# A gated recurrence computed in two halves of channel blocks, with its gate products, exponentials and the next projection in another order

## The reference

```python
u, g = jnp.split(h @ w_in, 2, axis=-1)
u = causal_depthwise_conv(u, conv_w) + conv_b          # 4 taps
r  = sigmoid(block_diag(u, w_a) + b_a)                 # forget gate
gi = sigmoid(block_diag(u, w_x) + b_x)                 # input gate
log_a = -8.0 * r * softplus(-lam)
a = exp(log_a)
b_in = sqrt(-expm1(2.0 * log_a)) * (gi * u)
hs = scan over tokens of  h = a * h + b_in
x = x + gate * ((hs * silu(g)) @ w_out)
```

## Time and profile before

| | us |
|---|---|
| median of 3 runs | 1071.15 |
| the runs | 1072.08, 1065.59, 1071.15 |
| the profiled execution | 1070.5 |
| its span, first to last instruction | 1068.7 |
| PE busy | 950.9 (89%) |
| DVE busy | 751.5 (70%) |
| ACT busy | 469.9 (44%) |
| POOL busy | 96.6 (9%) |

### The profile page before, as it was taken

How to read it: one execution, slowest core, us unless ns; L and a number is a source line. 1 busy time by engine, 2 the same in 40 slices (tenths; PEclk the granted TensorE clock), 3 DMA queues, 4 the chain that set the end, 5 groups by cost and what they waited for, 6 DMA issues and landing times.

```text
span 1068.7 us, 12457 instructions
## 1 busy us (share of the span) xinstructions
PE 950.9 (89%) x4385; PEld 744.1 (70%) x4385; DVE 751.5 (70%) x1061; ACT 469.9 (44%) x728; POOL 96.6 (9%) x134
## 2 busy tenths in 40 slices
PE   3799986989999999899887999999958968998986
PEld 1588664766888888676566788888747856776765
DVE  0697497688768777865388877677779397784464
ACT  1542356444343343443254443443455764544461
POOL 0000010113001000100030001010000400100000
PEclk8799998898999999899988999999989989999998
DMA  9977164267998889545025698998825353764001
GB/s 355 375 258 255 40 224 147 82 228 253 343 323 286 310 292 303 189 145 155 3 80 197 232 344 290 309 295 297 313 79 197 110 191 133 261 250 158 1 1 40
DMA packets 115814, 222.91 MB, mean 209 GB/s; under 512 B 7146, under 2 KB 63180, under 8 KB 115770
## 3 DMA queue, kind: packets, MB, share of 16 engines
q1 hardware_dynamic: 92608, 141.57, 38.3%
q0 software_dynamic: 20992, 80.13, 22.0%
q10 hardware_dynamic: 2170, 0.64, 0.3%
HBM read 221.27 MB, written 1.05 MB: 208 GB/s over the span
## 4 chain that ended last, share of the span: by engine, by line
PE 71%; DVE 15%; ACT 5%; issue 4%; DMA 2%; POOL 1%; ACTq 0%; POOLq 0%; DVEq 0%; SPq 0%
PE bank L1668 20%; PE bank L1670 19%; PE bank L1669 19%; DVE w_lo L1016 4%; ACT w_hi L533 2%; DMA w_land<-ev_w_in_dram 2%; DVE job_sum L1033 1%; PE bank L2195 1%; PE bank L1725 1%; DVE tmp L1103 1%; DVE x L1104 1%; PE bank L1894 1%; PE bank L2029 1%; POOL x L489 1%; DVE xfull L1142 1%
## 5 line engine op out<-in xcount | busy, mean ns | idle before, releaser
L1668 PE MATMUL bank<-w_hi,xT_hi 128*128 128x512 f32 x816 | 337.9, 414 | 31.6 <-DVE xT_lo L1126 14.1
L1016 DVE TENSOR_TENSOR w_lo<-w_land,w_hi 128x2048 fp32r<-128x2048 f32 x124 | 283.4, 2289 | 99.0 <-ACT w_hi L533 98.7
L1669 PE MATMUL bank<-w_lo,xT_hi 128*128 128x512 f32 x816 | 326.8, 401 | 0.0
L1670 PE MATMUL bank<-w_hi,xT_lo 128*128 128x512 f32 x816 | 326.4, 400 | 0.0
L533 ACT ACTIVATE w_hi<-w_land 128x2048 fp32r<-128x2048 f32 x124 | 236.9, 1912 | 135.2 <-PE bank L1670 132.0
L1668 PEld LDWEIGHTS bank<-w_hi,xT_hi 128*128 128x128 f32 x816 | 159.1, 195 | 72.6 <-issue 27.5
L1670 PEld LDWEIGHTS bank<-w_hi,xT_lo 128*128 128x128 f32 x816 | 158.7, 194 | 35.1
L1669 PEld LDWEIGHTS bank<-w_lo,xT_hi 128*128 128x128 f32 x816 | 159.4, 195 | 32.2 <-issue 1.0
L1033 DVE SCALAR_TENSOR_TENSOR job_sum<-a_land,silu_c,job_sum 128x1024 f32<-128x1024 f32 x126 | 164.2, 1303 | 6.6 <-DMA a_land<-mod_w_dram 3.1
L1668 PE MATMUL bank<-w_hi,hT_hi 128*128 128x512 f32 x176 | 70.4, 400 | 1.0 <-DVE w_lo L1016 1.0
L1670 PE MATMUL bank<-w_hi,hT_lo 128*128 128x512 f32 x176 | 68.7, 390 | 0.0
(11 more groups left out here) (291 smaller groups left out, 1051.3 us busy)
## 6 DMA issues: line engine op xcount, KB each, us to landing
...
```

The costliest lines, as they stand in the source:

```text
L1016: dve.tensor_tensor(w_lo[u % N_SPLIT][:, :], w_land[n % N_LAND][:, :], w_hi[u % N_SPLIT][:, :].bitcast(F32), ALU.subtract).then_inc(s_lo, 1)
L1668: pe.matmul(dst, hi, whi, start=start, stop=False)
L1669: pe.matmul(dst, hi, wlo, start=False, stop=False)
L1670: return pe.matmul(dst, lo, whi, start=False, stop=stop)
```

## The change

- The four groups of the forget gate come first in RG_GROUPS, then the four of the input gate.
- The eight exponentials follow the second pair of forget groups. The input gate is computed as tanh of half the argument, with a halved bias (half_bias, one small DVE instruction), in place of a sigmoid; DVE forms (tanh+1)*uc, and the root is taken of a quarter of its argument, which brings the missing half.
- POOL no longer multiplies the input gate by uc, and squares a for all eight blocks; DVE squares none.
- The silu of chunk 2 is applied as it leaves the banks. `split_hi` of base+9 comes before `rg_rows(3)`.
- DVE and ACT take blocks 0 to 3 through root product, scan, silu product and split, then the gate's diagonal, then blocks 4 to 7, with `split_lo` of base+9 between their scans and their outputs.
- PE does the first unit of rg_out for tile 0 before the transposes of chunk 3, tile 1 after them. Writing banks 4 and 5 in `gate_mm` waits for the last silu.

```diff
-RG_GROUPS = [(0, 0), (0, 1), (1, 0), (1, 1), (0, 2), (0, 3), (1, 2), (1, 3)]
+RG_GROUPS = [(0, 0), (0, 1), (0, 2), (0, 3), (1, 0), (1, 1), (1, 2), (1, 3)]
...
         sp_c = small("sp_c", [P, 8, KT])
+        half_bias = place("half_bias", [P, KT], FOUR_G)
...
             for k in range(KT):
-                pool.wait_ge(sem("rg_sig"), rg_sigs(1, k))
-                pool.tensor_tensor(i_gate[:, k, :], i_gate[:, k, :], uc[:, k, :], ALU.mult).then_inc(sem("rg_iu"), 1)
-            for k in range(0, KT, 2):
                 pool.wait_ge(sem("rg_a"), k + 1)
...
                     k = 2 * h + e
-                    dst, b = ((r_gate, "rg_b_a_2"), (i_gate, "rg_b_x_2"))[n]
-                    act.activation(dst[:, k, :], bank[6 + g % 2][:, 256 * e:256 * e + 256], ACT.Sigmoid,
-                                   bias=pc(b, k)).then_inc(sem("rg_sig"), 1)
+                    src = bank[6 + g % 2][:, 256 * e:256 * e + 256]
+                    if n == 0:
+                        ins = act.activation(r_gate[:, k, :], src, ACT.Sigmoid, bias=pc("rg_b_a_2", k))
+                    else:
+                        ins = act.activation(i_gate[:, k, :], src, ACT.Tanh, scale=0.5, bias=half_bias[:, k:k + 1])
+                    ins.then_inc(sem("rg_sig"), 1)
                 if n == 0:
...
             split_hi(base + 7)
-            for g in range(2, 6):
+            for g in range(2, 4):
                 rg_sigmoids(g)
+            for k in range(KT):
+                act.wait_ge(sem("rg_th"), k + 1)
+                act.activation(r_gate[:, k, :], r_gate[:, k, :], ACT.Exp, scale=sp_c[:, 7, k:k + 1]).then_inc(sem("rg_a"), 1)
+            act.wait_ge(sem("half_bias"), 1)
+            rg_sigmoids(4)
+            rg_sigmoids(5)
             rg_rows(2)
...
             rg_sigmoids(7)
-            rg_turned(2)
-            for k in range(KT):
-                act.wait_ge(sem("rg_th"), k + 1)
-                act.activation(r_gate[:, k, :], r_gate[:, k, :], ACT.Exp, scale=sp_c[:, 7, k:k + 1]).then_inc(sem("rg_a"), 1)
             split_hi(base + 8)
...
                 act.wait_ge(sem("rg_m"), k + 1)
-                act.activation(b_seq[:, k, :], b_seq[:, k, :], ACT.Sqrt, scale=-1.0).then_inc(sem("rg_sqrt"), 1)
+                act.activation(b_seq[:, k, :], b_seq[:, k, :], ACT.Sqrt, scale=-0.25).then_inc(sem("rg_sqrt"), 1)
+            rg_turned(2, ACT.Silu)
+            act.wait_ge(s_used, base + 7)
+            full_hi("rg", y_full, xT_hi, range(4))
+            split_hi(base + 9)
             rg_rows(3)
-            act.wait_ge(sem("rg_turned"), 6)
-            for k in range(0, 4, 2):
-                act.activation(gT[:, k:k + 2, :], gT[:, k:k + 2, :], ACT.Silu).then_inc(sem("rg_g"), 1)
             rg_turned(3, ACT.Silu)
-            split_hi(base + 9)
-            full_hi("rg", y_full, xT_hi)
+            for k in range(4, KT):
+                act.wait_ge(*seen("full", "rg", k + 1))
+                act.activation(xT_hi[:, k, :], y_full[:, k, :], ACT.Copy).then_inc(sem("hi"), 1)
             dense_out("rg_out", "n_kv", 16)
...
             tile_operand("n_rg", xfull, xT_hi, xT_lo, V_MOD0, AFTER_FFN, (), BASE["rg_in"] + 2, NT)
+            dve.tensor_scalar(half_bias[:, :], pc("rg_b_x_2", 0, KT), 0.5, None, ALU.mult).then_inc(sem("half_bias"), 1)
             dve.wait_ge(sem("ru_zero"), 1)
...
             for k in range(KT):
-                if k % 2 == 0:
-                    dve.wait_ge(sem("rg_a2"), k // 2 + 1)
-                else:
-                    dve.wait_ge(sem("rg_a"), k + 1)
-                    link(dve.tensor_tensor(y_full[:, k, :], r_gate[:, k, :], r_gate[:, k, :], ALU.mult))
+                dve.wait_ge(sem("rg_a2"), k + 1)
                 dve.scalar_tensor_tensor(out=b_seq[:, k, :], in0=y_full[:, k, :], scalar=1.0, in1=b_seq[:, k, :],
                                          op0=ALU.add, op1=ALU.mult).then_inc(sem("rg_m"), 1)
+            for k in range(KT):
+                dve.wait_ge(sem("rg_sig"), rg_sigs(1, k))
+                dve.scalar_tensor_tensor(out=i_gate[:, k, :], in0=i_gate[:, k, :], scalar=1.0, in1=uc[:, k, :],
+                                         op0=ALU.add, op1=ALU.mult).then_inc(sem("rg_iu"), 1)
             split_lo(base + 8)
-            dve.wait_ge(sem("rg_iu"), KT)
-            for k in range(KT):
-                dve.wait_ge(sem("rg_sqrt"), k + 1)
-                dve.tensor_tensor(i_gate[:, k, :], i_gate[:, k, :], b_seq[:, k, :], ALU.mult).then_inc(sem("rg_b"), 1)
-                if k >= 1:
-                    rg_scan(k - 1)
-            rg_scan(KT - 1)
...
-            for k in range(KT):
-                dve.wait_ge(sem("rg_h"), k + 1)
-                dve.wait_ge(*((sem("rg_g"), k // 2 + 1) if k < 4 else (sem("rg_turned"), 7 + (k - 4) // 2)))
-                dve.tensor_tensor(y_full[:, k, :], uc[:, k, :], gT[:, k, :], ALU.mult).then_inc(sem("full"), 1)
-                if k >= 1:
-                    rg_low(k - 1)
-            rg_low(KT - 1)
+            def rg_states(ks):
+                for k in ks:
+                    dve.wait_ge(sem("rg_sqrt"), k + 1)
+                    dve.wait_ge(sem("rg_iu"), k + 1)
+                    dve.tensor_tensor(i_gate[:, k, :], i_gate[:, k, :], b_seq[:, k, :], ALU.mult).then_inc(sem("rg_b"), 1)
+                    if k > ks[0]:
+                        rg_scan(k - 1)
+                rg_scan(ks[-1])
+            def rg_outputs(ks):
+                for k in ks:
+                    dve.wait_ge(sem("rg_h"), k + 1)
+                    dve.wait_ge(sem("rg_turned"), 5 + k // 2)
+                    dve.tensor_tensor(y_full[:, k, :], uc[:, k, :], gT[:, k, :], ALU.mult).then_inc(sem("full"), 1)
+                    if k > ks[0]:
+                        rg_low(k - 1)
+                rg_low(ks[-1])
+            rg_states(range(4))
+            rg_outputs(range(4))
+            gate_diag("rg_out", mc(V_MOD0 + 2))
+            rg_states(range(4, KT))
             split_lo(base + 9)
-            gate_diag("rg_out", mc(V_MOD0 + 2))
+            rg_outputs(range(4, KT))
             mod_cols(pc("kv_norm_g_2", 0, KT), V_KV + 1)
...
                 def mid():
+                    if stage == "rg_out":
+                        pe.wait_ge(sem("rg_turned"), 8)
                     gate_mm(stage)
...
                             unit_wait(u + j)
-                            half(u + j, j, xT_hi, xT_lo, banks, s_used, ready if c == 0 else None,
+                            begun = (stage, c, j) == ("rg_out", 0, 0)
+                            half(u + j, j, xT_hi, xT_lo, banks, s_used, ready if c == 0 else None, range(begun, NT),
                                  part=parts and n_chunks == 2)
...
                 n, h = RG_GROUPS[g]
-                if g in (0, 2):
+                if g in (0, 4):
                     pe.wait_ge(sem(f"rg_w{n}"), 16)
...
                         job_sums(15)
+                if c == 3:
+                    unit_wait(BASE["rg_out"])
+                    half(BASE["rg_out"], 0, xT_hi, xT_lo, bank[0:2], None, "rg", (0,))
                 turn_pair("rg_in", rg_tok, rg_free)(c)
...
                     rg_gate_mm(1)
-            pe.wait_ge(sem("rg_in_tok"), 8)
-            pe.wait_ge(sem("rg_turned"), 8)
             pe.wait_ge(sem("rg_sig"), 2 * KT)
```

## The result

| | before | changed |
|---|---|---|
| median of the four runs each, side by side | 1071.62 | 1058.09 |
| the runs | 1065.59 to 1074.82 | 1057.01 to 1059.28 |
| profiled execution, span | 1068.7 | 1057.1 |

The ratio on record is 0.9897, 95% interval 0.9869 to 0.9925: 11.0 us faster, between 8.0 and 14.0. The two medians lie 13.5 us apart, near the upper end of that interval. A second set of runs of the changed kernel gave 1058.25 against 1069.16, ratio 0.9915 (0.9883 to 0.9947). The forecast of 1061.5 was 3.4 us above the measured 1058.09; the range of 1057 to 1067 held.

The account below looks back on a forecast made before the run. PE was held by a 6.80 us wait for DVE's late xT_lo, then a low clock. Gain 10.5 less 1.2 is 9.3 us; 1070.5 profiled becomes 1061.2, plus half the difference to the median: 1061.5, range 1057 to 1067.

Parts of the forecast that it names:

- The rest of the norm hangs on DVE and shifts with it: Norm behind the output projection: after the wait ahead of the normed tile's transposes, the remainder moves along with DVE.
- 1.2 us given back: Behind the output projection: DVE's late residuals open a 1.3 to 1.7 us PE wait, costing 1.2 us of the gain.
- the sum: Whole change: 10.5 us gained in the output projection less 1.2 lost at the normed tile, 9.3 us faster.
- about 2.8 is the low clock: Output projection: 14 matmuls at 0.43 us instead of 0.227 account for about 2.8 us of the 10.5 gained.
- the 10.5: Output projection: its 24 matmuls of the second half end at 870.1 instead of 880.65, a gain of 10.5 us.
- B: Norm ahead of the key/value stage: a second low-clock stretch vanishes too, 1.7 us more, 1059.8; chance 0.20.
- C: Output projection: shorter PE waits still lower the clock for as long, 2.8 us return, 1064.3; chance 0.21.
- D: DVE through both halves: handoffs add tenths, PE's second half and the residual slip up to 5 us, 1066.5; chance 0.11.
- E: POOL's squares ahead of DVE's unit split set the pace: 4.7 us slower, 1075.2; chance 0.03.

Follow-up runs that it names:

- the early copy: Changed kernel with ACT's copy of unit base+10 moved ahead of the last four xT_hi copies; 1059.68 against 1068.48 us, ratio 0.9914, stage 65.25.

## Why the prediction was right, step by step

**Right: what bound, and what would take its place.** Squares were to end 22.7 us into the stage and ended at +22.5 (839.08); DVE's last product at +23.1, measured +23.1; the first xT_lo of the second half freed PE at +45.9 instead of +46.3; the projection's second column chunk began at +51.5 instead of +51.8. The wait ahead of the normed tile was 1.11 us, said to be 1.3 to 1.7. Each came within 0.4 us. The likely reason is that the durations were taken with their handoffs, from rows of the same engines doing the same pairs of steps; no run tests that.

**Mis-sized by 0.7 us: "The rest of the norm hangs on DVE and shifts with it", with 1.2 us given back.** The two kernels' second column chunks begin at +62.4 and +51.5, a gain of 10.9 (880.67 - 818.29 less 868.05 - 816.57). At the transposes of the normed tile it is 72.07 - 62.43 = 9.6, so 1.3 has indeed been given back. But from there to the first waiting key/value matmul the kernel before took 4.10 us and the changed one 3.39, so 0.71 came back. Before, DVE's split of base+13 waited 0.73 us for ACT's copy (891.03), and ACT 0.60 for PE (889.09). In the changed kernel PE was ahead of DVE, ACT's copy was done in time, and DVE split without a wait:

```profile
878.96 2.29 DVE L1021 TENSOR_TENSOR w_lo<-w_land,w_hi 128x2048 fp32r<-128x2048 f32 x1
```

The runs without early matmuls and with the early copy show the 4.10 again (67.29 - 63.19, 65.25 - 61.15), as soon as PE no longer waits for the normed tile. So of the 1.05 us by which the stage's gain beat the sum, 0.7 is this and the rest is 0.4 us of earlier starts in the second half.

**Wrong in its reason: "about 2.8 is the low clock".** The stage of the kernel before at full clock was 0.4 us shorter, not 2.8. Beside the slow matmuls stood DVE's unit split and diagonal, which held PE's second unit nearly as long; the changed kernel moves both ahead of the outputs of blocks 4 to 7. The low clock was worth 0.4 by itself and 2.1 together with the diagonal; how the 10.5 divides beyond that isn't shown. The sum came out right since it went by when PE's second unit could start, which holds under either reason; the split into causes was read off the clock alone.

**The 3.4 us between 1061.5 and 1058.09.** 1.05 is the stage. 1.7 lies ahead of it, less 0.5 behind it. The last 1.1 is how the profiled executions lie to the medians: the changed kernel's took 0.7 us more than its median, and the forecast had added 0.3 for the kernel before. The 1.7 fits the clock: summed over windows of 1 us, the lower level held for 81.9 us ahead of the stage in the one profile and 78.5 in the other. It was in no term of the sum, so that part of the miss is chance.

**The rivals.** B did not happen in the profile: behind the waits of the norm, the longest of 2.57 us, the changed kernel is at the lower level for 3.4 us (893 to 897), as the earlier trace rows had it. It is no property of the kernel, though. The run with the sigmoid, whose stage is the same, has none there:

```profile
893.00:897.00 4.00, 4.00 (x13) 3.10 (x12) 2.89 (x11) 1.68 (x6) 0.00 (x0) 0.57 0.75 252
```

```profile
892.00:897.00 5.00, 4.71 (x21) 3.90 (x22) 3.66 (x14) 3.59 (x8) 0.00 (x0) 1.00 0.66 210
```

C did not happen: waits up to 1.11 us left the clock at full in both profiles of the changed kernel. So did 2.46 us in the run without early matmuls, but in one profile, which proves little, since a wait of 2.57 in the norm went with a fall in some profiles and not in others. What a low stretch there would have cost was not run. D did not: DVE's handoffs were as measured. E's mechanism is real, as the doubled squares show, but its pace was 0.71 a square against the 1.85 it needed (by its own sum 1.85 makes DVE 6.2 us late, not 6.5; the pace that breaks even is 1.89).

By the rule of the Trainium skill, SBUF — State Buffer (the shared port pair), a DVE instruction with two SBUF inputs and a GpSimd one that reads SBUF exclude each other, which I took to mean 1.1 us a block. The eight blocks took 0.71 each. Both engines are held back, each by less than the other's whole instruction. In the changed kernel the first two squares, begun before any product, take 0.61 and 0.60 us and start 0.58 apart; the other six take 0.79 and start 0.75 apart. Seven products take 0.82 or 0.83; the last, beside no square, 0.41. If each waited for the other's whole instruction, a block would take their sum, at least 1.0. The trace doesn't bear that out, and the measured pace decides.
